# State-space scan taken group of heads by group, with the output product's tiles between its steps

## What is computed

```python
def mamba2_mixer(h, norm_w, in_w, conv_w, conv_b, dt_bias, a_log, d_skip, gnorm_w, out_w):
    zxbcdt = rms_norm_2(h, norm_w) @ in_w
    z, xbc, dt = jnp.split(zxbcdt, [D_INNER, D_INNER + CONV_CH], axis=-1)   # 2048, 3072, 32 columns
    xbc = jax.nn.silu(causal_conv4(xbc))
    xs, bm, cm = jnp.split(xbc, ...)          # 2048, 4 groups x 128, 4 groups x 128
    dt = jax.nn.softplus(dt + dt_bias)
    y = ssd_chunked(xs, dt, -jnp.exp(a_log), bm, cm)      # 32 heads of 64, 2 chunks of 128 rows
    y = (y + d_skip[:, None] * xs).reshape(b, s, D_INNER) * jax.nn.silu(z)
    yg = y.reshape(b, s, SSM_GROUPS, D_INNER // SSM_GROUPS)
    yg = yg * lax.rsqrt(jnp.mean(yg * yg, axis=-1, keepdims=True) + EPS)   # norm over one group's 512 columns
    return (yg.reshape(b, s, D_INNER) * gnorm_w) @ out_w
# in ssd_chunked, for one chunk and one head, a_cum = cumsum(dt * a):
#   y_diag[i] = sum_{j<=i} (cm_i . bm_j) exp(a_cum_i - a_cum_j) x_j dt_j
#   y_off[i]  = exp(a_cum_i) (cm_i . state of the chunk before)
```

## Time and profile before

| | us |
|---|---|
| median of 3 runs (1156.23 to 1160.98) | 1156.68 |
| the profiled execution, whole | 1150.49 |
| its span on the core | 1148.7 |
| PE busy / DVE / ACT in it | 977.0 / 714.0 / 498.6 |
| the mixer, first xbc matmul to the end of the products behind "so" (627.5 to 918.0) | 290.5 |

### The profile page before, as it was taken

How to read it: one execution, slowest core, us unless ns; L and a number is a source line. 1 busy time by engine, 2 the same in 40 slices (tenths; PEclk the granted TensorE clock), 3 DMA queues, 4 the chain that set the end, 5 groups by cost and what they waited for, 6 DMA issues and landing times.

```text
span 1148.7 us, 14272 instructions
## 1 busy us (share of the span) xinstructions
PE 977.0 (85%) x5745; PEld 848.8 (74%) x5745; DVE 714.0 (62%) x977; ACT 498.6 (43%) x681; POOL 61.5 (5%) x65
## 2 busy tenths in 40 slices
PE   4899999999875959997995999788828987989887
PEld 4788898898754759997784999667616866767666
DVE  4478627935775368898346786644573567875463
ACT  4654322334522346665234555422252446545451
POOL 6002303400000000000000000000000000000000
PEclk9899999999988979999896998887968998989899
DMA  8343122224524325665352455311103543520050
GB/s 273 117 141 106 42 74 74 74 74 132 198 74 147 110 92 185 201 202 184 121 193 90 148 156 179 110 37 37 48 25 119 183 147 122 191 100 1 4 181 37
DMA packets 80226, 135.77 MB, mean 118 GB/s; under 512 B 3845, under 2 KB 46177, under 8 KB 80032
## 3 DMA queue, kind: packets, MB, share of 16 engines
q1 hardware_dynamic: 78336, 131.37, 34.8%
q0 software_dynamic: 1824, 3.48, 1.0%
HBM read 133.79 MB, written 1.05 MB: 117 GB/s over the span
## 4 chain that ended last, share of the span: by engine, by line
PE 58%; DVE 12%; ACT 7%; issue 4%; DVEq 0%; ACTq 0%
PE bank L415 16%; PE bank L416 15%; PE bank L417 15%; PE bank L403 3%; ACT upper L1025 3%; DVE lower L1419 2%; PE bank L903 1%; DVE arena L1911 1%; DVE arena L1861 1%; PE bank L880 1%; PE bank L800 1%; ACT arena L1070 1%; PE bank L888 1%; DVE arena L1923 1%; DVE arena L1455 1%
## 5 line engine op out<-in xcount | busy, mean ns | idle before, releaser
L1419 DVE TENSOR_TENSOR lower<-loaded,upper 128x2048 fp32r<-128x2048 f32 (+1 forms) x123 | 279.8, 2276 | 208.7 <-ACT upper L1025 207.2
L1025 ACT ACTIVATE upper<-loaded 128x2048 fp32r<-128x2048 f32 (+1 forms) x123 | 233.7, 1901 | 239.8 <-PE bank L417 230.7
L415 PE MATMUL bank<-xT_upper,upper 128*128 128x256 f32 x656 | 187.1, 285 | 13.2 <-DVE xT_lower L1463 12.9
L416 PE MATMUL bank<-xT_lower,upper 128*128 128x256 f32 x656 | 185.4, 283 | 0.0
L417 PE MATMUL bank<-xT_upper,lower 128*128 128x256 f32 x656 | 185.2, 282 | 0.0
L415 PE MATMUL bank<-upper,xT_upper 128*128 128x512 f32 (+1 forms) x368 | 154.0, 418 | 9.4 <-DVEq L1476 7.2
L416 PE MATMUL bank<-lower,xT_upper 128*128 128x512 f32 (+1 forms) x368 | 146.9, 399 | 0.0
L417 PE MATMUL bank<-upper,xT_lower 128*128 128x512 f32 (+1 forms) x368 | 146.3, 397 | 0.0
L415 PEld LDWEIGHTS bank<-xT_upper,upper 128*128 128x128 f32 x656 | 127.0, 194 | 15.3 <-issue 14.6
L415 PE MATMUL bank<-upper,split_arena 128*128 128x512 f32 x296 | 120.0, 405 | 19.6 <-DVE split_arena L1825 7.5
L403 PE MATMUL bank<-consts,arena 128*128 128x128 f32 (+2 forms) x333 | 60.5, 338 | 81.3 <-DVE arena L1444 29.6
(11 more groups left out here) (305 smaller groups left out, 1246.9 us busy)
## 6 DMA issues: line engine op xcount, KB each, us to landing
loaded<-in_w_in SPq DMA_DIRECT2D x27, 1024.0 KB, 5.2
loaded<-in_ffn_w_up SPq DMA_DIRECT2D x22, 1024.0 KB, 5.1
loaded<-in_ssm_in_w SPq DMA_DIRECT2D x20, 1024.0 KB, 5.3
loaded<-in_ffn_w_down SPq DMA_DIRECT2D x11, 1024.0 KB, 4.9
loaded<-in_ssm_out_w SPq DMA_DIRECT2D x8, 1024.0 KB, 4.9
loaded<-in_ple_gate_w SPq DMA_DIRECT2D x8, 1024.0 KB, 5.1
loaded<-in_attn_in_w SPq DMA_DIRECT2D x8, 1024.0 KB, 5.2
loaded<-in_w_branch_ret SPq DMA_DIRECT2D x4, 1024.0 KB, 4.9
```

The source lines that it names most:

```text
L415: mm(out, a[0], b[0], start=start, stop=False)
L416: mm(out, a[0], b[1], start=False, stop=False)
L1025: A(part(upper, PARTS, n), part(loaded, LOADS, n), ACT.Copy).then_inc(uppers, 1)
L1419: TT(part(lower, LOADS, n), part(loaded, LOADS, n), part(upper, PARTS, n).bitcast(F32), sub) \
```

## The change

- The scan runs group by group, `STEPS` = (g, n, half): four steps make one group (two chunks, two halves of four heads).
- PE: at step z it spreads step z+2, then does one piece of 12 matmuls: the eight quarter pieces of z2 and z3 in steps 0 to 7 and tiles 0 to 7 of "so" in steps 8 to 15. Tiles 8 to 11 follow the loop, the last group's transposes, then tiles 12 to 15.
- `spread` begins with one more matmul, a 512-column mask product that adds -2^100 times (1 - incl) where j > i; with it ACT takes the exponential straight out of PSUM, with -a_cum as its bias. DVE's four subtractions per step go, ACT has four exponentials of 128 columns instead of one of 512. `cb` is copied by ACT without its mask.
- Per group: gate, squares, root, scaling, transposes, norm weights. `silu(z)` is taken when z leaves PSUM. Norm weight and rounding are one ACT instruction of 128 columns (8 per group), norm weight and subtraction one DVE instruction of 128 columns (8 per group).
- `dt` moves between xbc5 and xbc6, the transposes of x after xbc3, 5, 7 and 9, and the `ac` sums after xbc8. The small DVE and ACT work for dt moves among the channels (`step_sizes`, `step_logs`, `step_sums`).
- z0 and z1 are cut into quarters around bR, cb and the states; `postw` and `lora` are reused as space; POOL's load of `p_2` waits for the gate and not for the transposed rows.

```diff
-    turned("xbc", "ssm_in_w_2", 2048, 3072)
+    turned("xbc", "ssm_in_w_2", 2048, 1536)
     out.append(("dt", "ssm_in_w_2", 0, KT, 5120, 32))
+    turned("xbc", "ssm_in_w_2", 2048, 3072, 6)
...
+        STEPS = [(g, n, hf) for g in range(4) for n in range(2) for hf in range(2)]
...
+            def x_turns(q):
+                pe.wait_ge(sem("xbc_ready"), 4 * q + 4)
+                for i in range(2):
+                    turns(("xsT", i, q), 4 + 2 * (q % 2) + i, [xbc[:, 4 * q + j, P * i:P * i + P] for j in range(4)])
             for j in range(12):
                 turned(f"xbc{j}", [("xbc", 2 * j), ("xbc", 2 * j + 1)], (2 * (j % 2), 2 * (j % 2) + 1),
                        2 if j == 0 else None)
+                if j in (3, 5, 7, 9):
+                    x_turns((j - 3) // 2)
...
+                if j == 8:
+                    pe.wait_ge(sem("adt_ready"), 1)
+                    ps = take(pe, ("ac",), 6)
...
+            def spread(z):
+                g, n, hf = STEPS[z]
+                ps = take(pe, ("bc", z), 4 + z % 2)
+                mm(ps[:, :].rearrange("p (a b) -> p a b", a=4), masks[:, 0, :],
+                   masks[:, 1, :].unsqueeze(1).broadcast_to([P, 4, P]), start=True, stop=False)
...
+            for z, (g, n, hf) in enumerate(STEPS):
+                if z + 2 < 16:
+                    spread(z + 2)
+                if z % 4 == 2 and g:
+                    group_turns(g - 1, 0)
+                if z < 8:
+                    z_piece(*GATES[z])
+                else:
+                    out_tile(z - 8)
+                if z % 4 == 2 and g:
+                    group_turns(g - 1, 1)
+                if hf:
+                    diagonal(g, n)
+                if z % 4 == 2:
+                    carried(g)
+            for t in range(8, 12):
+                out_tile(t)
+            for i in range(2):
+                group_turns(3, i)
+            out_tile(12)
...
-            for u in range(16):
-                act.wait_ge(sem("seg_ready"), u + 1)
-                A(eT2[:, u % 2, :], eT2[:, u % 2, :], ACT.Exp).then_inc(sem("seg_exp"), 1)
...
+            for z, (g, n, hf) in enumerate(STEPS):
+                ps = full(act, ("bc", z))
+                if z >= 2:
+                    act.wait_ge(sem("wT_ready"), z - 1)
+                for e in range(4):
+                    hd = 8 * g + 4 * hf + e
+                    ins = A(eT2[:, z % 2, P * e:P * e + P], ps[:, P * e:P * e + P], ACT.Exp, bias=nacs[:, n, hd:hd + 1])
+                empty(ins, ("bc", z))
+                if z in SPLIT:
+                    split_to(*SPLIT[z])
+                if z == 4:
+                    z_gate(2)
+                if z % 4 == 0 and g:
+                    group_squares(g - 1, 0)
+                if z % 4 == 1 and g:
+                    group_squares(g - 1, 1)
+                    group_root(g - 1)
+                if z % 4 == 2 and g:
+                    group_upper(g - 1, 0)
+                    group_upper(g - 1, 1)
+                if z == 7:
+                    z_gate(3)
...
+                if c == 11:
+                    step_sizes()
+                if c == 14:
+                    step_logs()
+                if c == 19:
+                    step_sums()
```

More of the change, by code:

```diff
@@ L76, in weight_units, with turned @@
     out = []
[L78 to L79 removed]
+    def turned(name, w, c0, cols, first=0):
+        for j in range(first, cols // 256):
             out.append((f"{name}{j}", w, 0, KT, c0 + 256 * j, 256))
@@ L266, in build @@
         ss0 = ar(0, 4, 512)
-        yg = ar(2048, 2, 4, 512)
-        ygT = two(16384, 20480, 16, T)
+        ygT = [two(6144 + 2048 * b, 7168 + 2048 * b, 4, T) for b in range(2)]
         prow, pT = ar(2048, 2, T), two(2560, 3072, 2, T)
@@ L765, in _ @@
-            turns(("bR",), 6, [xbc[:, 16 + g, 0:P] for g in range(4)])
-            rows("z1", z_keys(1), (2, 3), xT)
-            for n in range(2):
-                ps = take(pe, ("cb", n), 7)
+                if j in (3, 5, 7, 9):
+                    x_turns((j - 3) // 2)
+                if j == 5:
+                    ps = take(pe, ("dt",), 4)
+                    w = unit("dt")
+                    for i in range(2):
+                        for k in range(KT):
+                            last = mm3(ps[:, 32 * i:32 * i + 32], both(xT, every, k, slice(i * P, i * P + P)),
+                                       both(w, every, k, every), k == 0, k == KT - 1)
+                    fill(last, ("dt",))
+                    used("dt", key=("dt",))
@@ new lines, in diagonal, with carried @@
+            def diagonal(g, n):
+                pe.wait_ge(sem("wT_ready"), 4 * g + 2 * n + 2)
+                ps = take(pe, ("yd", g, n), 6 + n)
+                for e in range(8):
+                    hd = 8 * g + e
+                    last = mm(ps[:, 64 * e:64 * e + 64], wT[:, n, e, :], xd[:, n, 64 * hd:64 * hd + 64],
+                              start=True, stop=True)
+                fill(last, ("yd", g, n))
+            def carried(g):
+                emptied(pe, ("sst", g))
+                ps = take(pe, ("yo", g), 6)
+                fill(mm(ps[:, :], xbc[:, 20 + g, P:2 * P], ss0[:, g, :], start=True, stop=True), ("yo", g))
@@ L769, in _ @@
+            z_piece(0, 0, 0)
+            z_piece(0, 0, 1)
+            pe.wait_ge(sem("xbc_ready"), 24)
+            turns(("bR",), 5, [xbc[:, 16 + g, 0:P] for g in range(4)])
+            z_piece(0, 1, 0)
+            z_piece(0, 1, 1)
+            for n in range(2):
+                ps = take(pe, ("cb", n), 6 + n)
                 for g in range(4):
@@ L812, in _ @@
-            pe.wait_ge(sem("yg_rows"), 2)
+            z_piece(1, 0, 0)
+            z_piece(1, 0, 1)
+            emptied(pe, ("bR",))
+            pe.wait_ge(sem("xd_ready"), 2)
+            states(0)
+            states(1)
+            z_piece(1, 1, 0)
+            states(2)
+            states(3)
+            z_piece(1, 1, 1)
+            pe.wait_ge(sem("masks_ready"), 1)
+            spread(0)
+            spread(1)
+            pe.wait_ge(sem("xd_ready"), 3)
+            GATES = [(j, half, i) for j in (2, 3) for half in range(2) for i in range(2)]
```

400 lines of the change are left out of this document (210 added, 190 removed).

## The result

The changed kernel takes 1124.78 us (1120.93 to 1126.45), the kernel before in the same comparison 1157.34 (1156.23 to 1160.98): a ratio of 0.971, 95% interval 0.968 to 0.974. The profiled execution of the changed kernel took 1124.57 us, with a span of 1122.8.

A forecast was written before the change was run, and what follows sets the result against it. PE's work and its 48.1 us of waits, plus a lowered scan clock, were taken to bound the mixer; 246.1 - 1.5 + 7.0 + 2.3 + 7 + 4 = 264.9 us, 25.6 less than 290.5, giving 1131 us, range 1114 to 1150.

The forecast's parts named there:

- wait 1: End of xbc9: PE waits for DVE to empty bank 6 behind the unit's tail; 7.0 us, bounds 5 and 8.
- wait 2: Ahead of bR, which needs all 24 channels: PE waits for the last channel; 2.3 us, bounds 1 and 4.
- wait 3: Inside the loop: PE sets the pace, handoffs to ACT and DVE cost 7 us, bounds 2 and 20.
- wait 4: Behind the loop: last group's norm hidden by tiles 8 to 11, its transposes wait 4 us, bounds 2 and 6.
- PE work other than 246: Sign of a wrong forecast in the mixer's profile: PE work was put at 242.4 + 3.7 = 246.1 us.
- net -1.5: Mixer's clock: half of the scan's 9.7 us won, 3.4 us lost behind the bank 6 wait.
- ACT sets the pace: Rival, in the loop: half of ACT's handoffs show, three groups cost 20 us for 7; 1144 us, chance 0.20.
- the same list and starts earlier: Behind the mixer, from h joined onward: the work is unchanged and only begins sooner.
- Smooth: Rival, in the mixer: handoffs hide and the clock stays at full level; 1113, halfway 1118 us; chance 0.15.
- Costly loads: Rival: a drain-like pause at each of 12 table loads, 1.4 us more each, 17 us; 1148 us, chance 0.05.
- Slower by coupling: Rival: coupling between loop steps; gain gone at 32.6 us of loop waits; 1166 us at 42; chance 0.07.
- Doesn't do what it says: Rival: units of the loop's tiles come late, so PE waits there for what it saved; 1157 us, chance 0.03.

The follow-up runs named there:

- the two repeats: The changed kernel run again unaltered, as the base of two batches: 1121.27 us (ratio 0.973 to the kernel before) and 1119.71 us (0.971).
- the experiment: Changed kernel with the transposes behind xbc9 in banks 4 and 5, leaving bank 6 to the sums; run twice: 1112.51 us (0.966) and 1111.80 us (0.963).
- the two profiles above: Changed kernel with five moves together (bank 6, bR, tile 11, embedding transposes, z2's gate): 1104.73 us; the same without the gate move: 1112.21 us.
- the loads run: Changed kernel with one more Exp and Sqrt of 128x1 behind each of three roots in the loop, six more table loads: 1131.91 us, ratio 0.980.

## Why the prediction was right, and where its terms were off

The prediction was 1131 us in 1114 to 1150, and faster at 0.89; it came to 1124.8. Its terms for the mixer, beside what the first profile after shows:

| term | predicted | measured | read from |
|---|---|---|---|
| PE work with the clock | 244.6 | 233.4 | stretches |
| wait 1, bank 6 | 7.0 | 9.4 | waits |
| wait 2, bR | 2.3 | 2.3 | waits |
| wait 3, in the loop | 7 | 9.3 | 6.2 + 2.7 + 0.4 |
| wait 4, behind the loop | 4 | 3.6 | 2.5 + 1.1 |
| other | 0 | 0.5 | the rest of 25.1 |
| mixer | 264.9 | 258.5 | |
| outside the mixer, against before | 0 | +6.1 | stretches |
| own time of the profiled execution | 1124.9 | 1124.6 | |

The own time agrees to 0.3 us, and only because two errors of 6 us cancel, the mixer and what lies outside it. Inside the mixer errors cancel too: PE's work was put 11.2 us too high, its waits 4.8 us too low. That the sum came so near is luck, and so is part of the agreement with this one profile: the two repeats have 251.0 and 254.3 us for the mixer, 14 and 11 under the forecast. The prediction's own list of what would be wrong has "PE work other than 246", and that sign came. The last 6.2 us of the forecast, the step from the profiled execution to the median, didn't apply: the profiled execution of before lay 6.2 us under its median (1150.5 and 1156.7), that of after lies on it (1124.57 and 1124.78). That offset is chance of one execution.

**PE's own work: 11.2 us too much** (16 and 21 in the repeats). The step that failed is the clock's, "net -1.5". Without it the forecast has 246.1, the profile 233.4, so that 12.7 us came back where 1.5 were put down. Two things were wrong. "I take half of the 9.7 as won" was one: the loop ran at 0.95 here and at 1.00 in a repeat. The other is that 9.7 was the loss in the scan's stretch alone, while the other stretches have losses too: 0.88, 0.64 and 0.97. Taking each stretch's PE busy time by its missing clock, before has 2.8 + 5.8 + 9.7 + 2.2 + 1.6 = 22.1 us, after 4.8 + 5.2 + 4.4 + 0 = 14.4: 7.7 us won. That leaves 5.0 of the 12.7 which this account doesn't place; a stretch's clock is a mean in which idle time counts too. The diagonals show how the low clock hid in a price. For the length of a group each had been taken at an eighth of 20.3; by line and form over the mixer after (busy us, mean ns, idle before) they are

```profile
L810 PE MATMUL bank<-arena 128*128 128x64 f32 x128 | 15.1, 271 | 0.0
L797 PE MATMUL bank<-masks 128*128 128x512 f32 x16 | 8.0, 499 | 6.2 <-ACT arena L1387 6.2
```

5.2 us less for the same 64 matmuls (128 rows). Two of the eight blocks before, with the carried part behind each, and one of after:

```profile
797.02 3.47 PE L800 MATMUL bank<-arena 128*128 128x64 f32 x16 [2.02 <-DVE arena L1923]
800.29 2.02 PE L806 MATMUL bank<-arena 128*128 128x512 f32 x2
...
811.73 2.00 PE L800 MATMUL bank<-arena 128*128 128x64 f32 x16 [1.23 <-DVE arena L1923]
813.56 1.08 PE L806 MATMUL bank<-arena 128*128 128x512 f32 x2
```

```profile
789.72 1.89 PE L810 MATMUL bank<-arena 128*128 128x64 f32 x16
```

The block of 3.47 stands where the carried part takes 2.02, the one of 2.00 where it takes 1.08, the lower and the full level. Four blocks before were of the first kind (3.07, 3.17, 3.47, 2.69), four of the second (2.00 three times, 1.89). In the loop after, all eight are 1.89. Behind wait 1, 3.4 us were put down as lost at the low level, where the rows show 1.9. The mean of a row was used where its single rows fell in two classes: the four slow blocks are 4.8 us over 1.9 each, and these 4.8 us of clock stand in the 242.4 of PE's work that the sum starts from. The mask product's 3.7 is neither confirmed nor refuted: issued twice it cost 2.2 us by time and nothing in the mixer of the profile.

**Wait 1: 9.4 for 7.0.** The step that failed is "they are late by about 1 us". ACT's copy started 3.0 us after PE's unit ended (698.3 to 701.3), so the taps and reads ended 3 us late, not 1. The upper bound had been 8, so it was too low as well. What made ACT 3 us late and not 1 was not taken apart. That PE waits at this bank, for this reader, and that it was a matter of the bank alone, was as forecast, and the experiment shows it.

**Wait 2, bR:** 2.3 as forecast. With bank 6 free it is 0.7, so it was in part an effect of wait 1.

**Wait 3: 9.3 for 7.** Both places are the ones named: exponentials ahead of a spread, and the second transposes behind bank 7. No wait is over 2.3 us. What was wrong is the reasoning that ACT had 8 us to spare in each group. It has them in the group as a whole, not at the root: 8.9 us put there came out as 6.7 us of waits. The loads behind the first root are mostly covered, those behind the other two are not. So the rival "ACT sets the pace" had the right mechanism and the wrong size: 9.3 us in the loop, 3.1 per group, where it said 6 to 7 per group and 20.

**Wait 4: 3.6 for 4.** In two parts: 2.5 for bank 7, where 2.3 was forecast, and 1.1 for the lower part. The norm of the last group hides behind tiles 8 to 11, as said.

**Behind the mixer: "the same list and starts earlier" failed.** There is a wait that was not there before:

```profile
889.29 1.97 PE L408 MATMUL bank<-consts,arena 128*128 128x128 f32 x16 [1.72 <-DVE arena L1553]
```

The embedding's transposes now have 48 matmuls behind them where they had 60, and DVE's norm scaling for the next block ends behind PE instead of ahead. With these transposes one tile earlier the 1.7 us are gone. The other 4.4 us outside the mixer are the clock in code that isn't touched (0.93 for 0.94, 0.91 for 0.92), and executions of kernels with the same code there differ by more, 9 us ahead of the mixer in the two profiles above.

**The rivals.** "Smooth" (1118): the loop's waits did not hide, but the clock did stay up, and it gave back more than this rival's 9.7 us. Its 1118 is not halfway between its 1113 and the forecast, which is 1122; by that number the measured 1124.8 lies nearer to it than to 1131. "ACT sets the pace" (1144), as above. "Costly loads" (1148): refuted by the rows of the loads run. "Slower by coupling" (1166): waits of 9.3 us in the loop where it needed over 32.6. "Doesn't do what it says" (1157): in the loop PE never waits for weights.

## What to carry to other kernels

When tiles are moved between steps of a serial loop, read the price of the steps' matmuls from single rows without a wait ahead of them, and look at the granted clock in the loop: here four tiles taken out of the loop cost 5.5 us of PE's work at a lower clock and 3.6 by waits. Cut every profile at the same instructions before stretches are compared: the mixer of the changed kernel started at 629.1, 631.0 and 633.2 us in three executions. An engine's slack over a group says little where its work has one serial spot; put the extra cost at that spot to see what it has. And every small product that takes a bank between two large ones should be checked for who reads it and what stands ahead of that reader: here another bank for one set of transposes was worth 9 us.

## What the runs showed of the hardware

- The granted clock in a loop of small f32 matmuls is 1.00 (one execution of the changed kernel) or 0.95 (two) with a dense piece of 12 matmuls in each step. In the last four steps it is 1.00 or 0.93 with the pieces, and 0.73 when these steps have none.
- A change of ACT's function costs 1.28 us of ACT for the load and 0.01 to 0.02 more, four in a row at one root included.
- Eight f32 matmuls of 64 columns (sixteen rows of the trace) take 1.89 us at the full clock without a wait ahead, 2.00 behind one, and 2.69 to 3.68 where the clock is at its lower level for part of them or all.
- ACT takes four exponentials of 128x128 from PSUM with a bias in 1.14 us, 0.285 each, the 0.3 of the forecast.
